# A hybrid attention layer: the output product moved to the end of the next tile, and the scale and shift of the input done token by token with a DMA transpose

## The chip, the cores and the metric

One NeuronCore of a Trainium2 chip runs the whole program. The metric is device microseconds of one execution. In the texts PE is TensorE (matrix products), DVE is VectorE, ACT is ScalarE, POOL is GpSimd, and SP is the engine whose queue issues the DMAs. A semaphore wait on an engine holds everything that stands behind it in that engine's program.

## What is computed

One layer over 4096 prompt tokens and 64 sample tokens, width 1024 (cut to what matters):

```python
shift, scale, gate = split(silu(c) @ w_ada + b_ada)
h = rmsnorm(x, g_pre) * (1 + scale) + shift
gq, gk, gv, gg, ga, sq, sk, sv, sg = split(h @ w_in)
o_gla = rmsnorm(gla_recurrence(q, k, v, log_a, S0), g) * silu(gg)
o_swa = sink_attention(rope(q), rope(k), v, window) * silu(sg)
o = concat(o_gla, o_swa) @ w_out
y = x + gate * rmsnorm(o, g_post)
```

## The kernel before

The prompt is cut into 32 tiles of 128 tokens (t = 0 to 31); tile 32 is the sample and step 33 only finishes it. Each engine has a `program(c)` that is run for each tile; tiles 0, 1 and 30 to 33 are written out, the rest is a loop over pairs of tiles (lines 251 to 259). All order is set by hand, by the order of instructions in each program and by semaphores.

Every large product is made of f16 halves: an operand is split into a high half (rounded to f16) and a low half (the rest), and `split_product` (line 425) adds high x high, high x low and low x high for each of the 8 chunks of the inner dimension: 24 matmuls at line 429. hT holds the two halves of h with channels on the partitions, for two tiles in turn. The products by h of a tile are qk (four blocks of 128), the 272-wide k/v/low-rank product into bank5, the SWA query product into bank7 and the GLA value product into bank6 (512 wide each), the GLA gate product gg into bank7 and the SWA gate product sg into bank6. The output product takes the mix of the previous tile and wo_hi, wo_lo: 48 matmuls into pairP.

PE's order in tile t (lines 492 to 646): qk of t; the GLA output and the state product of t-1 (lines 529 to 540); the 272-wide product; the product of probabilities and values of t-1 (PV, line 555); the query product; a small transpose of the low-rank part; the value product; z (line 578); the output product of t-1 (line 597); the scores (line 615); gg; eight transposes of the normalised x of tile t+1 into pairP (line 631); the transposes of k and the GLA block matrix A (lines 636 to 642); sg. So step t does the first half of tile t and the second half of tile t-1.

How h of tile t+1 comes about: ACT squares x and makes 1/rms (`x_stats`, line 667); POOL multiplies x by it into xs (`norm_x`, line 1131); PE transposes xs; DVE scales and shifts each of the eight channel blocks by columns of mod (`h_f32`, line 873), which also frees pairP; ACT writes the high half into hT (`h_hi`, line 700) and DVE the low half (`h_lo`, line 881).

The gates: ACT writes exp of the product into etmp, DVE adds 1, takes the reciprocal and multiplies by the product (lines 1091 to 1096 for gg, 1099 to 1111 for sg, both through the one buffer etmp). The softmax: DVE takes maxima of the scores (lines 1056 and 1057) and three small steps, ACT takes exponentials into late (line 811) and writes their high half into pair_tok (line 818), DVE the low half (line 1082). aT is lines 1076 to 1080. In line 1018 DVE copies a small column, in line 1060 it copies keys.

POOL (lines 1140 to 1199): copies of values, the rotary terms, `norm_x`, three GLA scalings, the residual add to y (line 1188), and a multiply of each gate half (lines 1193 and 1198).

SP's queue in order (lines 369 to 414): three DMA transposes of the mix from pair_tok into late (`turn_mix`), three of query and key halves (`turn_heads`), the store of y, a copy of x into x_res, the load of x for tile t+2, two transposes of the probabilities' halves (`turn_probs`). pair_tok carries first the mix, then the probabilities; the second half of late takes their transposes.

At the start, w_ada and w_in come in units through staging places, and ACT (`split_hi`) and DVE (`split_lo`) split each. The eight units of w_out pass through three places of stage (lines 53 and 112): units 0 to 2 are loaded in tile 0, units 3 to 5 behind tile 0's probabilities, 6 and 7 behind the mix of tile 1.

Of the kernel before, what the change touches and what calls it, by code (L numbers as in the profile page):

```python
# [12 lines left out]
P = 128  # L13
D = 1024
# [38 lines left out]
UNITS += [("out", i, 17 + i % 3) for i in range(OUT_UNITS)]  # L53
SLOTS = 20
SAME_PLACE = {17: (0, 17), 18: (1, 18), 19: (1, 19)}
# [16 lines left out]
class Tile:  # L72


    def __init__(self, t, half, par):
        peeled = isinstance(t, int)
        self.t, self.half, self.par = t, half, par
        self.prev = not (peeled and t == 0)
        self.cur = not (peeled and t == NT + 1)
        self.next = not (peeled and t >= NT)  # L80
        self.first = peeled and t == 0
        self.second = peeled and t == 1
        self.last = peeled and t == NT - 1
        self.sample = peeled and t == NT
        self.after = peeled and t == NT + 1


def hybrid_layer(nc, x_prompt, x_sample, c_prompt, c_sample, state_gla, cache_k, cache_v, w_ada, b_ada, g_pre,
# [3 lines left out]
    with ctx:  # L92
# [22 lines left out]
        gate_diag = y_buf[0].rearrange("p (c k) -> p c k", c=KC)  # L115
        first_diag = late[:, 0:D].rearrange("p (c k) -> p c k", c=KC)
        probs = late[:, 0:D].rearrange("p (g k) -> p g k", g=GROUPS)
        pair_tok = sb("pair_tok", [P, 2, D], F16)
        pair_ch = late[:, D:2 * D].bitcast(F16).rearrange("p (s c k) -> p s c k", s=2, c=KC)
# [7 lines left out]
        h_ch = xs[:, :].rearrange("p (c k) -> p c k", c=KC)  # L127
        hT = sb("hT", [P, 2, 2, KC, P], F16)
# [90 lines left out]
        u_ps = pairQ[:, 640:896].rearrange("p (b k) -> p b k", b=2)  # L219
# [14 lines left out]
        for name in ("c_load bg_load const_load c_t bg_t bg_ev rows_ev rows_t c_exp c_one c_rec c_silu eps_set "  # L234
                     "ident_z ident mask_z causal scan_z scan_m state_in gaT_one ga_lo w_al_hi w_al_lo mod_mm "
                     "mod_sum mod_out zeroed kcache_t cache_kA gdiag_d gate_bc gate_row x_sq x_lnd x_rs xs h_f32 "
# [29 lines left out]
        def _(sp):  # L266
# [58 lines left out]
            for n, (kind, i, slot) in enumerate(UNITS[:unit_number("out", 3)]):  # L325
# [43 lines left out]
            def program(c):  # L369
                if c.prev:  # L370
                    turn_mix(c)
                if c.second:
                    load_out((6, 7))
                if c.cur:
                    turn_heads(c)
                if c.last or c.sample:
# [7 lines left out]
                if c.prev:  # L384
                    sp.wait_ge(sem["y_final"], c.t)
                    src = y_buf[1 - c.par]
                    if c.after:
                        sp.dma_start(y_sample[0], src[0:DEC_SEQ, :]).then_inc(y_stored[1 - c.par], 16)
                    else:
                        sp.dma_start(y_prompt[0, bass.ds((c.t - 1) * P, P), :], src).then_inc(y_stored[1 - c.par], 16)  # L390
                if c.cur:
                    sp.wait_ge(x_loaded[c.par], 32 * (c.half + 1))
                    sp.dma_start(x_res[:, :], x_in[:, c.par, :]).then_inc(sem["res_copied"], 16)
                if not isinstance(c.t, int) or c.t + 2 <= NT:
                    sp.wait_ge(sem["res_copied"], 16 * (c.t + 1))
                    sp.wait_ge(sem["xs"], c.t + 1)
                    sp.wait_ge(sem["rope"], c.t + 1)
                    load_x(c.t + 2, c.par)
                if c.sample or c.after:
# [5 lines left out]
                if c.sample:  # L405
                    sp.wait_ge(sem["out_stored"], 16 * 4)
                    for q in range(2):
                        sp.dma_start(S[DK * q:DK * q + DK, :, q, :],
                                     state_gla[0, 0].rearrange("(b q) k v -> q k b v", q=2)[q])\
                          .then_inc(sem["state_in"], 16)  # L410
                if c.cur:
                    turn_probs(c)
                if c.first:
                    load_out((3, 4, 5))
# [9 lines left out]
        def _(pe):  # L424
# [58 lines left out]
            def gate_to_rows(count):  # L483

                pe.wait_ge(sem["gdiag_d"], count)
                diagonal = (first_diag, gate_diag)[count - 1]
# [3 lines left out]
                last.then_inc(sem["gate_bc"], 1)  # L490

            def program(c):
# [12 lines left out]
                if c.cur:  # L505
                    pe.wait_ge(sem["h_lo"], t + 1)
                    if c.first:
                        pe.wait_ge(sem["cache_kA"], 1)
                    else:
                        pe.wait_ge(sem["at_d"], t)  # L510
                    if c.first:
                        pe.wait_ge(w_split, in_units_before[W_QK])
# [6 lines left out]
                if c.prev:  # L519

                    pe.wait_ge(sem["at_d"], t)
                    pe.wait_ge(sem["gg_x"], t)
                    pe.wait_ge(sem["v_ev"], t)
                    if not c.second:
# [3 lines left out]
                    for b in range(2):  # L528
                        pe.matmul(bank7[:, 2 * b * DV:2 * (b + 1) * DV], q_int[:, b, :], S[:, b, :, :],
                                  start=True, stop=False)  # L530
                        for q in range(2):
                            o = slice((2 * b + q) * DV, (2 * b + q + 1) * DV)
                            last = pe.matmul(bank7[:, o], aT[:, b, q, :], v_tok[:, o], start=False, stop=(q == 1))
                    last.then_inc(sem["o_mm"], 1)

                    n = DEC_SEQ if c.after else P
                    pe.wait_ge(sem["p_exp"], t)
                    for hd in range(GH):
                        b, q = hd // 2, hd % 2
                        last = pe.matmul(u_ps[DK * q:DK * (q + 1), b, :], k_tok[0:n, b, DK * q:DK * (q + 1)],  # L540
                                         v_tok[0:n, hd * DV:(hd + 1) * DV], start=True, stop=True)
                    last.then_inc(sem["u_mm"], 1)
                if c.cur:
                    project(bank5, KSG, W_KSG, sem["ksg_mm"])
                if c.prev:
                    pe.wait_ge(sem["probs_dma"], 32 * t)
                    pe.wait_ge(sem["sg_x"], t)
                    pe.wait_ge(sem["v_keys"], t)
                    for g in range(KVH):
                        for ch in range(2):  # L550
                            v = vB[:, 1 - par, :, :] if ch else (vA_s if c.after else vA[:, 1 - par, :, :])
                            for pp in range(2):
                                k = 4 * g + 2 * ch + pp
                                for n, (i, j) in enumerate(((0, 0), (0, 1), (1, 0))):
                                    last = pe.matmul(bank6[:, k * HD:(k + 1) * HD], pair_ch[:, i, k, :],
                                                     v[:, j, HD * g:HD * (g + 1)], start=(n == 0), stop=(n == 2))
                    last.then_inc(sem["pv_mm"], 1)
                if c.cur:
                    if c.prev:
                        pe.wait_ge(sem["mix_gla"], t)  # L560
                    project(bank7, 512, W_SQ, sem["sq_mm"])
                    pe.wait_ge(sem["ksg_ev"], t + 1)
                    pe.wait_ge(sem["ga_lo"], t + 1)
                    pe.wait_ge(sem["vb_lo"], t + 1)
                    pe.transpose(gaT_ps, ga_pair[:, :], ident16[:, :]).then_inc(sem["gat_mm"], 1)
                if c.cur:
                    if c.first:
                        pe.wait_ge(sem["mod_sum"], 2)
                    if c.prev:
                        pe.wait_ge(sem["mix_swa"], t)  # L570
                    project(bank6, 512, W_V, sem["v_mm"])
# [8 lines left out]
                    last.then_inc(sem["z_mm"], 1)  # L580
                if c.prev:
                    pe.wait_ge(sem["mix_dma"], 48 * t)
                    if c.after:
                        pe.wait_ge(sem["gate_row"], 2)
                    else:
                        pe.wait_ge(sem["h_f32"], t + 1)
                    if c.second:
                        pe.wait_ge(w_split, len(IN_UNITS) + OUT_UNITS)

# [10 lines left out]
                if not c.cur:  # L600
                    return
                if c.first:
                    pe.wait_ge(sem["h_f32"], 1)
                    gate_to_rows(1)
                pe.wait_ge(sem["pair_dma"], 48 * (t + 1))
                pe.wait_ge(sem["k_ev"], t + 1)
                if c.prev:
                    pe.wait_ge(sem["s_upd"], t)
                for ch in range(2):
                    for pp in range(2):  # L610
                        for g in range(KVH):
                            kk = kB if ch else kA
                            head = 4 * g + 2 * pp
                            for part in range(2):
                                last = pe.matmul(scores[:, 4 * g + 2 * ch + pp, :],  # L615
                                                 qT[:, ch, head:head + 2, :], kk[:, g, part, :],
                                                 start=(part == 0), stop=(part == 1))
                last.then_inc(sem["sc_mm"], 1)
                pe.wait_ge(sem["sq_ev"], t + 1)
                project(bank7, 512, W_GG, sem["gg_mm"])  # L620
                if c.sample:
                    pe.wait_ge(sem["y_mul"], t)
                    gate_to_rows(2)
                if c.next:
                    pe.wait_ge(sem["xs"], t + 2)
                    if c.prev:
                        pe.wait_ge(sem["y_mul"], t)
                    else:
                        pe.wait_ge(sem["gate_row"], 1)
                    for cc in range(KC):  # L630
                        last = pe.transpose(pairP_c[:, cc, :], xs[:, cc * P:(cc + 1) * P], ident[:, :])  # L631
                    last.then_inc(sem["xt_mm"], 1)

                pe.wait_ge(sem["gla_sc"], t + 1)
                for b in range(2):
                    pe.transpose(kt_ps[:, b, :], k_out[:, b, :], ident[:, :])
# [600 lines left out]
```

## Time and profile before

| | us |
|---|---|
| three runs | 1714.31, 1716.46, 1716.52 (median 1716.46) |
| the profiled execution, its own time | 1715.52 |
| its span, first to last instruction | 1713.8 |
| PE busy | 1591.8 (93%) |
| DVE, ACT, POOL busy | 1079.0, 593.1, 365.1 |
| mean granted clock of PE | 0.983 |

Busy times are sums over an engine's instructions. A start in the timeline is when an instruction begins on its engine; matmuls overlap, so the next one begins before the last has ended, and the distance from start to start is what a stream of them costs. In brackets stands how long the engine was idle before an instruction, and what it waited for.

### The profile page before, as it was taken

How to read it: one execution, taken by the hardware profiler on the slowest of the kernel's cores; microseconds unless marked ns; L12 is line 12 of the kernel's file. 1: busy time of each engine (PE TensorE's matmuls, PEld its weight loads, DVE VectorE, ACT ScalarE, POOL GpSimd, SP SyncE). 2: the span in 40 equal slices, each digit the busy share in tenths (PEclk: the TensorE clock that was granted, in tenths of full speed). 3: DMA queues.
4: the chain of work that ended last, by engine and by line, in shares of the span. 5: the costliest groups of instructions: out<-in, count | busy, mean ns of one | idle time of the engine just before them, and what ended most of it. 6: DMA issues, size and time to landing. Idle time of an engine off the chain costs nothing.

```text
span 1713.8 us, 31107 instructions
## 1 busy us (share of the span) xinstructions
PE 1591.8 (93%) x12209; PEld 922.4 (54%) x12209; DVE 1079.0 (63%) x1937; ACT 593.1 (35%) x1812; POOL 365.1 (21%) x505
## 2 busy tenths in 40 slices
PE   8875999999999999999999999999999999999994
PEld 3442555555555555555555555555555555555552
DVE  0684676766666676766666676766666676776653
ACT  0543333333332333333332333333332333333331
POOL 0022222222222122222222121222222121222220
PEclk9988999999999999999999999999999999999997
DMA  8933232222212222222212222222221222222221
GB/s 262 333 87 81 72 72 61 59 70 71 71 47 45 71 71 62 61 68 71 71 50 42 71 71 63 62 65 71 71 54 40 68 71 64 62 64 65 62 53 36
DMA packets 242392, 128.96 MB, mean 75 GB/s; under 512 B 203709, under 2 KB 228758, under 8 KB 242358
## 3 DMA queue, kind: packets, MB, share of 16 engines
q1 hardware_dynamic: 242358, 128.51, 29.3%
q8 instruction: 22, 0.36, 0.1%
q14 instruction: 12, 0.10, 0.0%
HBM read 46.08 MB, written 17.56 MB: 37 GB/s over the span
## 4 chain that ended last, share of the span: by engine, by line
PE 54%; DVE 36%; SPq 3%; issue 3%; DMA 2%; ACT 2%; POOL 0%; DVEq 0%; ACTq 0%; POOLq 0%
PE bank L429 29%; PE pairP L429 20%; DVE etmp L1102 6%; DVE etmp L1094 6%; DVE xs L877 4%; DVE pair_tok L1082 2%; DVE gates L1109 2%; DVE hT L883 2%; DVE gates L955 2%; DVE etmp L1100 2%; PE pairQ L615 2%; SPq L310 2%; PE pairP L631 2%; DMA wo_lo<-in_w_in 1%; DVE aT L1076 1%
## 5 line engine op out<-in xcount | busy, mean ns | idle before, releaser
L429 PE MATMUL bank<-w_hi,hT 128*128 128x512 f16 (+1 forms) x2640 | 749.3, 360 | 8.5 <-DVE gates L955 8.1
L429 PE MATMUL bank<-w_lo,hT 128*128 128x512 f16 (+1 forms) x1320 | 474.7, 360 | 0.0
L429 PEld LDWEIGHTS bank<-w_hi,hT 128*128 128x128 f16 x2640 | 258.0, 98 | 265.9 <-DVE gates L955 11.9
L429 PE MATMUL pairP<-wo_hi,late 128*128 128x512 f16 x1056 | 323.3, 383 | 26.4 <-DVE wo_lo L865 17.2
L429 PE MATMUL bank<-hT,w_hi 128*128 128x128 f16 x2112 | 182.2, 220 | 29.5 <-DVE hT L883 24.4
L429 PE MATMUL pairP<-wo_lo,late 128*128 128x512 f16 x528 | 202.3, 383 | 0.0
L429 PEld LDWEIGHTS bank<-w_lo,hT 128*128 128x128 f16 x1320 | 129.3, 98 | 113.7 <-issue 0.6
L1033 DVE SCALAR_TENSOR_TENSOR stage<-pairP,y_r,stage 128x1024 f32<-128x1024 f32 x33 | 42.4, 1284 | 231.4 <-ACT y_r L665 231.4
L429 PEld LDWEIGHTS pairP<-wo_hi,late 128*128 128x128 f16 x1056 | 104.0, 98 | 153.3 <-issue 21.7
L429 PEld LDWEIGHTS bank<-hT,w_hi 128*128 128x128 f16 x2112 | 161.7, 98 | 45.3 <-DVE hT L883 40.1
L429 PE MATMUL bank<-hT,w_lo 128*128 128x128 f16 x1056 | 179.9, 220 | 0.0
L811 ACT ACTIVATE late<-pairQ,m_neg 128x128 f32<-128x128 f32 (+1 forms) x264 | 92.4, 375 | 140.5 <-DVE m_neg L1066 140.5
L1193 POOL TENSOR_TENSOR gates<-gates,gnorm 128x512 f32<-128x512 f32 x33 | 42.0, 1272 | 428.8 <-DVE gates L1096 428.8
L1188 POOL TENSOR_TENSOR stage<-stage,x_res 128x1024 f32<-128x1024 f32 x32 | 75.9, 2372 | 208.6 <-DVE stage L1033 208.6
L990 DVE TENSOR_TENSOR etmp<-qk_tok,etmp 128x512 f16<-128x512 f32 x33 | 22.8, 692 | 153.2 <-ACT junk L761 153.2
L1094 DVE RECIPROCAL etmp<-etmp 128x512 f32<-128x512 f32 x33 | 110.6, 3353 | 1.1
L1102 DVE RECIPROCAL etmp<-etmp 128x512 f32<-128x512 f32 x33 | 110.6, 3353 | 1.1
L1135 POOL TENSOR_TENSOR xs<-x_in,x_r 128x1024 f32<-128x1024 f32 x33 | 64.2, 1945 | 214.7 <-ACT x_r L663 214.7
L877 DVE TENSOR_SCALAR xs<-pairP,mod 128x128 f32<-128x128 f32 x264 | 87.1, 401 | 27.5 <-PE pairP L631 27.5
L429 PEld LDWEIGHTS bank<-hT,w_lo 128*128 128x128 f16 x1056 | 103.7, 98 | 0.0
L797 ACT ACTIVATE stage<-pairP 128x1024 f32<-128x1024 f32 x33 | 33.8, 1023 | 190.9 <-PE pairP L429 190.9
L832 ACT ACTIVATE etmp<-bank 128x512 f32<-128x512 f32 x33 | 19.7, 597 | 226.3 <-DVE gates L1096 226.3
(197 smaller groups left out, 2191.1 us busy)
## 6 DMA issues: line engine op xcount, KB each, us to landing
x_res<-x_in SPq DMA_DIRECT2D x33, 512.0 KB, 3.5
x_in<-in_x_prompt SPq DMA_DIRECT2D x32, 512.0 KB, 3.5
out<-stage SPq DMA_DIRECT2D x32, 512.0 KB, 2.7
w_hi<-in_w_ada SPq DMA_DIRECT2D x5, 1024.0 KB, 9.4
w_lo<-in_w_ada SPq DMA_DIRECT2D x5, 1024.0 KB, 13.2
wo_lo<-in_w_in SPq DMA_DIRECT2D x5, 1024.0 KB, 11.9
wo_hi<-in_w_in SPq DMA_DIRECT2D x3, 1024.0 KB, 12.4
late<-pair_tok SPq DMA_TRANSPOSE x165, 3.1
```

Of the source, the lines that this page charges most:

```text
L310: sp.dma_start(dst, src.rearrange("(c p) n -> p c n", p=P)).then_inc(staged[slot], 16)
L429: last = pe.matmul(out, a(c, i), b(c, j), start=(c == 0 and n == 0), stop=(c == KC - 1 and n == 2))
L615: last = pe.matmul(scores[:, 4 * g + 2 * ch + pp, :], qT[:, ch, head:head + 2, :], kk[:, g, part, :], start=(part == 0), stop=(part == 1))
L631: last = pe.transpose(pairP_c[:, cc, :], xs[:, cc * P:(cc + 1) * P], ident[:, :])
L811: act.activation(probs[:, g, 0:w], scores[:, g, 0:w], ACT.Exp, bias=m_neg[:, g:g + 1], scale=HD ** -0.5, accum_out=row_sum[:, g:g + 1])
L877: last = dve.tensor_scalar(h_ch[:, cc, :], pairP_c[:, cc, :], mod[:, KC + cc, cond:cond + 1], mod[:, cc, cond:cond + 1], ALU.mult, ALU.add)
L1033: dve.scalar_tensor_tensor(y_buf[1 - par], pairP[:, :], y_r[:, :], gate_row, ALU.mult, ALU.mult)\
L1094: dve.reciprocal(etmp[:, :], etmp[:, :]).then_inc(sem["gg_r"], 1)
L1102: dve.reciprocal(etmp[:, :], etmp[:, :]).then_inc(sem["sg_r"], 1)
L1135: pool.tensor_tensor(xs[:, :], x_in[:, par, :], x_r[:, par:par + 1].to_broadcast([P, D]), ALU.mult)\
L1188: pool.tensor_tensor(y_buf[1 - par], y_buf[1 - par], x_res[:, :], ALU.add).then_inc(sem["y_final"], 1)
L1193: pool.tensor_tensor(gg, gg, gnorm[:, :].unsqueeze(1).to_broadcast([P, GH, DV]), ALU.mult)\
```

## The change

Four things change together.

First, the order of step t on PE: qk of t, GLA output of t-1 (now into pairQ), the 272-wide product, the query product (into bank6), the small transpose, PV of t-1 (into pairQ), the state product of t-1, the value product (into bank7), z, gg (bank6), sg (bank7), scores, the k transposes and A, and last the output product of t-1. DVE and ACT programs are reordered to match: gg's gate stands before the maxima, sg's gate after aT, the y of t-2 is scaled at the start of the step, and x_stats of t+1 comes first on ACT.

Second, h of tile t+1 is made with tokens on the partitions. Three rows (scale, shift, gate), broadcast over the partitions, are made at the start by the diagonal product that made the gate row before; scale lies in xs, shift in stage. POOL makes h in three operations in late, ACT and DVE write its halves into pair_tok, and two DMA transposes put them into hT. Tile 32's h is still made by PE's transposes, in step 31.

Third, POOL and SP: `make_h` stands first in POOL's step, then the residual add of y of t-2, then the rotary terms and the value copies. SP's order is: store of y of t-2, x_res loaded from the input in HBM, transposes of h, of heads, load of x for t+2, transposes of the mix, and transposes of the probabilities, which wait for the output product.

Fourth, w_out's units pass through two places of stage instead of three, as shift takes the third. Units 0 and 1 are loaded in tile 0, and three more pairs in tile 1.

```diff
-UNITS += [("out", i, 17 + i % 3) for i in range(OUT_UNITS)]
+UNITS += [("out", i, 18 + i % 2) for i in range(OUT_UNITS)]
...
+        shift_row = stage[:, D:2 * D]
+        h_tok = late[:, 0:D]
+        scale_row = xs[:, :]
+        o_ps = pairQ[:, 0:512]
+        pv_ps = pairQ[:, 512:1024]
...
             def turn_probs(c):
+                if c.prev:
+                    sp.wait_ge(sem["out_mm"], c.t)
...
+            def turn_h(c):
+                for part, done in enumerate(("h_hi", "h_lo")):
+                    sp.wait_ge(sem[done], c.t + 2)
+                    if c.prev and part == 0:
+                        sp.wait_ge(sem["sg_mm"], c.t)
+                    sp.sem_inc(sem["h_turn"], 1)
+                    sp.dma_start_transpose(hT[:, 1 - c.par, part, :, :], pair_tok[:, part, :]).then_inc(sem["h_dma"], 16)
...
             def program(c):
+                if c.prev2:
+                    sp.wait_ge(sem["y_final"], c.t - 1)
+                    sp.dma_start(y_prompt[0, bass.ds((c.t - 2) * P, P), :], y_buf[c.par]).then_inc(y_stored[c.par], 16)
                 if c.prev:
-                    turn_mix(c)
...
+                        sp.dma_start(x_res[:, :], x_prompt[0, bass.ds((c.t - 1) * P, P), :])\
+                          .then_inc(sem["res_copied"], 16)
                 if c.second:
-                    load_out((6, 7))
+                    load_out((2, 3))
+                if c.next and c.prev and not c.last:
+                    turn_h(c)
                 if c.cur:
                     turn_heads(c)
+                if c.second:
+                    load_out((4, 5))
...
+                if c.prev:
+                    turn_mix(c)
+                if c.second:
+                    load_out((6, 7))
...
PE
-                    pe.wait_ge(sem["h_lo"], t + 1)
+                    if c.first or c.sample:
+                        pe.wait_ge(sem["h_lo"], t + 1)
+                    else:
+                        pe.wait_ge(sem["h_dma"], 32 * t)
...
+                    pe.wait_ge(sem["sq_ev"], t + 1)
+                    project(bank6, 512, W_GG, sem["gg_mm"])
+                    pe.wait_ge(sem["v_ev"], t + 1)
+                    project(bank7, 512, W_SG, sem["sg_mm"])
...
                 if c.prev:
                     pe.wait_ge(sem["mix_dma"], 48 * t)
...
+                        pe.wait_ge(sem["y_mul"], t - 1)
...
ACT
+            def h_tok_hi(c):
+                act.wait_ge(sem["h_f32"], c.t + 2)
+                if c.prev:
+                    act.wait_ge(sem["probs_dma"], 32 * c.t)
+                act.activation(pair_tok[:, 0, :], h_tok, ACT.Copy).then_inc(sem["h_hi"], 1)
...
+                    if c.next and not c.last:
+                        act.wait_ge(sem["h_dma"], 32 * (t + 1))
                     act.activation(mix_tok[:, :, 0, :], gates[:, :].rearrange("p (f k) -> p f k", f=2), ACT.Copy)\
...
DVE
+            def h_tok_lo(c):
+                dve.wait_ge(sem["h_hi"], c.t + 2)
+                dve.tensor_tensor(pair_tok[:, 1, :], h_tok, pair_tok[:, 0, :], ALU.subtract).then_inc(sem["h_lo"], 1)
...
POOL
+            def make_h(c):
+                t, par = c.t + 1, 1 - c.par
+                pool.wait_ge(sem["x_rs"], t + 1)
...
+                    pool.wait_ge(sem["p_lo"], t - 1)
+                pool.tensor_tensor(h_tok, x_in[:, par, :], x_r[:, par:par + 1].to_broadcast([P, D]), ALU.mult)\
+                    .then_inc(sem["xs"], 1)
+                pool.wait_ge(sem["xs"], t + 1)
+                pool.tensor_tensor(h_tok, h_tok, scale_row, ALU.mult).then_inc(sem["h_a"], 1)
+                pool.wait_ge(sem["h_a"], t)
+                pool.tensor_tensor(h_tok, h_tok, shift_row, ALU.add).then_inc(sem["h_f32"], 1)
```

## Rows read from the trace of the kernel before

**Rows 1.** The page's head.

```profile
span 1713.8 us, 31107 instructions
```

**Rows 2.** Windows, one steady tile: stretch, length, busy of each engine, granted clock, DMA.

```profile
805.65:853.78 48.13, 46.39 (x363) 27.23 (x364) 31.41 (x58) 16.97 (x54) 10.88 (x15) 1.00 0.26 64
```

**Rows 3.** Timeline of PE in that tile: start, length, instruction, idle before.

```profile
816.19 0.28 PE L429 MATMUL bank<-w_hi,hT 128*128 128x272 f16 x1
817.20 0.34 PE L555 MATMUL bank<-vA,late 128*128 128x64 f16 x6 [0.73 <-issue]
...
818.31 0.39 PE L429 MATMUL bank<-w_hi,hT 128*128 128x512 f16 x1 [0.25 <-DVE gates L955]
...
829.37 0.39 PE L429 MATMUL pairP<-wo_hi,late 128*128 128x512 f16 x1
...
839.74 0.61 PE L615 MATMUL pairQ<-kA,qT 128*128 128x128 f16 x8
...
845.81 1.04 PE L631 MATMUL pairP<-ident,xs 128*128 128x128 f32 x8
846.68 0.38 PE L636 MATMUL bank<-ident,la 128*128 128x128 f32 x2
...
852.64 0.38 PE L429 MATMUL bank<-w_hi,hT 128*128 128x512 f16 x1
853.78 0.28 PE L429 MATMUL bank<-hT,w_hi 128*128 128x128 f16 x2 [0.76 <-DVE hT L883]
```

**Rows 4.** Timeline of DVE, the same tile and the seam behind it.

```profile
832.69 1.87 DVE L1018 COPY fac_in<-bsum 128x2 f32<-128x2 f32 x1
...
843.02 0.68 DVE L1056 TENSOR_REDUCE smax<-pairQ 128x4 f32<-128x512 f32 x1
...
846.01 0.17 DVE L1068 TENSOR_TENSOR sink_d<-sinks,m_neg 128x8 f32<-128x8 f32 x1
...
849.45 0.40 DVE L1076 TENSOR_TENSOR aT<-bank,causal 64x256 f32<-64x256 f32 x1
...
851.36 1.23 DVE L1082 TENSOR_TENSOR pair_tok<-late,pair_tok 128x1024 f16<-128x1024 f32 x1
...
859.16 0.91 DVE L1100 TENSOR_SCALAR etmp<-etmp 128x512 f32<-128x512 f32 x1 [0.72 <-ACT etmp L832]
...
865.26 1.13 DVE L955 SCALAR_TENSOR_TENSOR gates<-bank,o_r,gates 128x128 f32<-128x128 f32 x4
```

**Rows 5.** Timeline of POOL there.

```profile
832.59 1.94 POOL L1135 TENSOR_TENSOR xs<-x_in,x_r 128x1024 f32<-128x1024 f32 x1 [6.04 <-ACT x_r L663]
...
843.27 2.34 POOL L1188 TENSOR_TENSOR stage<-stage,x_res 128x1024 f32<-128x1024 f32 x1 [6.43 <-DVE stage L1033]
...
865.30 1.04 POOL L1198 TENSOR_TENSOR gates<-gates,rden 128x512 f32<-128x512 f32 x1 [5.52 <-DVE gates L1109]
```

**Rows 6.** SP's queue: two transposes, and the landing of those at line 355.

```profile
872.25 2.58 SPq L347 DMA_TRANSPOSE late<-pair_tok  x2
...
DMA to landing us min/median/max: 3.0/3.3/5.1
```

**Rows 7.** Timelines of start and end: PE, SP's queue and ACT.

```profile
143.77 2.40 SPq L317 DMA_DIRECT2D stage<-in_w_out  x4
...
150.74 1.06 ACT L689 ACTIVATE wo_hi<-stage 128x1024 f16<-128x1024 f32 x1 [1.15 <-DMA stage<-in_w_out]
...
153.19 0.59 PE L429 MATMUL pairP<-wo_hi,late 128*128 128x512 f16 x1 [17.16 <-DVE wo_lo L865]
...
179.92 0.28 PE L429 MATMUL bank<-hT,w_hi 128*128 128x128 f16 x2 [0.76 <-DVE hT L883]
...
1623.90 0.29 PE L429 MATMUL bank<-hT,w_hi 128*128 128x128 f16 x2 [0.76 <-DVE hT L883]
...
1664.06 1.88 PE L488 MATMUL pairP<-stage,causal 128*128 128x512 f32 x4
...
1692.53 0.61 PE L429 MATMUL pairP<-wo_hi,late 128*128 128x512 f16 x1 [9.27 <-DMA late<-pair_tok]
```

More of the change, by code:

```diff
@@ new lines, in program @@
+                    for ch in range(2):
+                        for pp in range(2):
+                            for g in range(KVH):
+                                kk = kB if ch else kA
+                                head = 4 * g + 2 * pp
+                                for part in range(2):
+                                    last = pe.matmul(scores[:, 4 * g + 2 * ch + pp, :],
+                                                     qT[:, ch, head:head + 2, :], kk[:, g, part, :],
+                                                     start=(part == 0), stop=(part == 1))
@@ L599, in program @@
                     last.then_inc(sem["out_mm"], 1)
[L600 to L632, printed above, removed]
@@ L800, in program @@
-                if not c.cur:
-                    return
-                if c.first:
-                    split_hi([("in", 11)])
-                act.wait_ge(sem["m_neg"], t + 1)
-                if c.prev:
-                    act.wait_ge(sem["p_lo"], t)
-                if c.first:
-                    act.wait_ge(sem["zeroed"], 1)
-                for g in range(GROUPS):
-                    w = CHUNK if c.first and g % 4 < 2 else P
-                    act.activation(probs[:, g, 0:w], scores[:, g, 0:w], ACT.Exp, bias=m_neg[:, g:g + 1],
-                                   scale=HD ** -0.5, accum_out=row_sum[:, g:g + 1])
@@ new lines, in program @@
+                    act.wait_ge(sem["m_neg"], t + 1)
+                    if c.last:
+                        act.wait_ge(sem["xt_mm"], 2)
+                    elif c.sample:
+                        act.wait_ge(sem["p_lo"], t)
+                    else:
+                        act.wait_ge(sem["h_lo"], t + 2)
+                    if c.first:
+                        act.wait_ge(sem["zeroed"], 1)
+                    for g in range(GROUPS):
+                        w = CHUNK if c.first and g % 4 < 2 else P
+                        act.activation(probs[:, g, 0:w], scores[:, g, 0:w], ACT.Exp, bias=m_neg[:, g:g + 1],
+                                       scale=HD ** -0.5, accum_out=row_sum[:, g:g + 1])
@@ new lines, in program @@
+                    act.wait_ge(sem["sink_d"], t + 1)
+                    act.activation(sink_e[:, :], sink_d[:, :], ACT.Exp).then_inc(sem["p_exp"], 1)
+                    act.wait_ge(sem["p_exp"], t + 1)
+                    if c.prev:
+                        act.wait_ge(sem["mix_dma"], 48 * t)
+                    else:
+                        act.wait_ge(sem["h_dma"], 32)
+                    act.activation(pair_tok[:, 0, :], late[:, 0:D], ACT.Copy).then_inc(sem["p_hi"], 1)
+                    if c.first:
+                        split_hi([("out", 0), ("out", 1)])
@@ L1111, in program @@
-                last.then_inc(sem["sg_x"], 1)
             all_tiles(dve, program, 2)
```

524 lines of the change are left out of this document (283 added, 241 removed).

## The prediction

> **What bounds the kernel now.** I read the profile's page first: a span of 1713.8 us [rows 1]. Its own time is 1715.52 us, so 1.7 lie around the span; it is 0.9 below the median of 1716.46, and I work against 1715.5. Then one steady tile by windows: 48.13 us, TensorE (PE) busy 46.39, VectorE (DVE) 31.41, ScalarE (ACT) 16.97, GpSimd (POOL) 10.88, granted clock 1.00 [rows 2]. PE is the bound; no other engine is near. Tile 2 begins at 179.92 and tile 32 at 1623.90 [rows 7]: 30 tiles of (1623.90 - 179.92) / 30 = 48.13. What a tile saves counts thirty times.
>
> Then PE's timeline of such a tile, to see what in 48.13 isn't products. It stands still three times: 0.73 before PV (L555), 0.25 before the SWA query product, 0.76 before the next tile's first product [rows 3], 1.74 in all. Each is more from start to start, as the pipe drains too. The 48 products of the output product start over 839.74 - 829.37 = 10.37 us, 0.216 each; the last gate product starts at 852.64 and could be followed at 852.86, but the next comes at 853.78: 0.92. The 272-wide product takes 0.115 apiece in proportion, so 816.30 to 817.20 is 0.90. Add 0.41 for the third (its 0.25 and a like drain). Sum 2.23. All three wait for DVE: at the tile's seam stands its gate chain, 6.10 long (859.16 to 865.26, [rows 4]) and there twice, which holds the banks and the gates.
>
> **The change, part by part.** *PE, removed.* Eight transposes of x, 846.68 - 845.81 = 0.87 a tile [rows 3]. Everything else is the same products in another order.
>
> *PE, the stalls.* T is the start of a tile's first product. Without stalls a tile is 48.13 - 2.23 - 0.87 = 45.03. The low end of the stalls by the tags alone, 1.74, gives 45.52. I take 45.05, as the drain is lost only when PE really waits. Is the new order free of waits? It ends with the output product, 10.37 long, so that starts at T+34.7. Ahead of it lie kt and A (first gate product 852.64 - 23 x 0.216 = 847.67, less 846.68: 0.99) and the scores (845.81 - 24 x 0.216 = 840.63, less 839.74: 0.89). So the last gate product ends at T+32.8 and the scores at T+33.7: 11.3 us of products cover what used to be the seam.
>
> *DVE behind that.* From T+33.7: maxima and their small successors 846.18 - 843.02 = 3.16 (with the waiting copy in it), aT 1.91 (849.45 to 851.36), the gate chain 6.10, then the probabilities' low half 1.23 [rows 4]. Finished at T+44.8 (gates) and T+46.1, which is 1.0 into the next tile. The next tile first needs those gates for its value product at T+16.7 and the transposed low half for PV at T+15.4. The h halves and aT are needed at T and T+5.4 of the next tile and are there many microseconds before. So the three stalls go, and I find none in their place on this side. h as eight DVE operations per tile goes too; it costs nothing in either kernel, as DVE has 16 us to spare a tile.
>
> *The new chain.* h of tile t+1 is now POOL, ACT, DVE, two DMA transposes; pair_tok holds it, then the mix, then the probabilities. POOL's gate multiply (1.04) ends at T+2.4; then x times 1/rms (1.95) and two products with a full second operand (2.35 each by the residual add, [rows 5]): T+9.1. The y add follows, T+11.4; before, it stood after the GLA scaling. ACT takes the high half after the k/v evictions: PE's 272-wide product ends at T+10.1 (816.30 - 805.65 less 0.6 for the state product moved behind PV), so T+10.7 to 11.8 with 1.06, as L689, of the same shape, takes [rows 7]. DVE's low half, 1.2, is done at T+13.0. SP is queued behind POOL's y add: y store and x_res load are issued at T+11.5 to 12.3, then two transposes at 1.29 each [rows 6]. The second goes out at T+13.6 and lands 3.3 later, T+16.9 (worst seen 5.1: T+18.7). ACT's mix high half waits for that, and the head split behind it on ACT, and the value eviction behind that; the value product ends only at T+22.0. PE does the query product (5.2), the small transpose and PV (0.7) after T+10.1, so PV ends at T+16.1 and its DVE multiply at T+16.8: the mix would not be there earlier anyway. Mix high half T+18.0, low half T+19.2, head low halves T+20.3. SP: three head transposes until T+24.2, the x load 0.8, three mix transposes, the last issued at T+27.6 and landing at T+30.9. The output product wants it at T+34.7: 3.8 to spare. With both landings at their worst (1.8 more each) 0.2 is left. I take no cost; ends are 0 and, if landings are all at the worst and 1 us more is lost in the queue, 0.8 a tile. The GLA scaling (qk_d at T+27) and the scores' heads (T+26) have 5 and more.
>
> *DMA.* Two more transposes a tile, 10 instead of 8, and x_res comes from HBM, no more than it took before; SP issues for some 15 of 45 us. Hidden.
>
> *The port.* DVE's copy L1018 is 1.87 long under POOL's x multiply (832.59 to 834.53), while four gate multiplies from PSUM run at their usual 1.13 beside POOL's 1.04 [rows 4, 5]. So some DVE operations wait for a POOL one to end and some don't. The Trainium skill, SBUF - State Buffer, section "SBUF: two separate sides", says that the port pair is locked for a whole instruction, and that a DVE operation with two SBUF inputs loses it to GpSimd as well. The trace agrees for L1018; the rule speaks against the change, which gives POOL 4.7 us more a tile. In the times above, POOL's block T+2.4 to 11.4 meets only DVE work that reads PSUM, and L1018 and the k copy fall free of POOL. If the block slips onto h's or the mix's low half, 2.35 a time is lost in the chain with 3.8 to spare.
>
> *Tile 31* keeps its PE transposes: 0.9 back.
>
> *The start.* Weights bound it. Before, the output product of tile 1 waited 17.16 for wo_lo [rows 7]. Now that product stands later in its tile, but w_out passes through two staging places instead of three, and the loads stand behind h and head transposes on SP. Tile 1 starts at about 112 as before. By the same durations (estimates, each step from the one before): tile 0's last gate multiply on POOL 123.9, h on POOL 130.7, h halves 133, splits of units 0 and 1 135.5, loads 2 and 3 with h's transposes 142, splits 146.4, head transposes 151.3, loads 4 and 5 (7.0 from first issue to both landed, 143.77 to 150.74, [rows 7]) 158, splits 160, loads 6 and 7 167, last split 169.6, output product 180. ACT blocks on the staged units, so the value eviction and the last gate product wait there too. Tile 2 at 180 against 179.92: 0, with ends of -10 (half of the stall saved) and +10 (one more round of 7 and a slow clock).
>
> *The tail.* From 1623.90 to the end 89.9. Now: the tile without stalls 45.05, probability transposes 4.7, PV and multiply 1.4, mix halves 3.4, three mix transposes 5.3, shift of the gate row (1.88, [rows 7], and a copy of 1) 3: output product at 62.9; after it 1713.8 - 1692.53 = 21.3 as before: 84.2. Saves 5.7.
>
> **Sum.** 30 x (48.13 - 45.05) = 92.4, less 0.9, plus 5.7, start 0: 97. 1715.5 - 97 = 1618.5; I say **1619**. The stalls at the tags' size alone: 30 x 0.47 = 14 more, 1633.
>
> **Rivals.** *A, no waits left on PE* (above): 1605 to 1640. For it: every wait in the new order has microseconds of cover. Against it: the chain through five units is longer than any now. Chance 0.68.
>
> *B, the h and mix chain is late by a little:* the output product stands 1 to 2 us in each tile, 1619 + 30 to 60 = 1649 to 1679. For: SP's fixed order puts h behind the y add. Against: 3.8 spare. 0.12.
>
> *C, POOL and DVE block each other:* by the rows' mechanism POOL's 9 us block slides under the low halves and each lengthens the other; two such waits of 2.35 are 4.7, less 3.8 spare is 0.9 a tile: 1646. The Trainium skill (SBUF - State Buffer, the same section) would have it so wherever these operations meet. 0.08.
>
> *D, slower:* the two added transposes, behind 1 MB of store and load, land late in every tile. The price is what exceeds 3.8; it outweighs the gain of 3.1 only from 6.9 us on. At 9 a tile costs 5.2 - 3.1 = 2.1 more than before: 1715 + 63 = 1778. Against: the probability transposes go out right behind an x load and land in 3.3, 5.1 at most [rows 6]. 0.07.
>
> *E, the change doesn't do what it says:* the seam's waits come back elsewhere at the same size (DVE's gate chain before the value product, say), and only the transposes are saved: 30 x 0.87 = 26, 1689; with the start at +10 and a chain 0.5 late, no change. 0.05, of which 0.02 ends within 0.2%.
>
> **How the numbers follow.** A measurement can tell some 0.2% (3.4 us) from no change. Faster: A, B, C and most of E, 0.91; same 0.02; slower 0.07. The range takes A with both bounds of start and stalls, C and the near half of B: 1604 (start -10, tail 5 better) to 1662. Outside lie the rest of B, D and E, under 0.2.
>
> **What would show it.** Right: PE's tile at 45.0 to 45.5, no idle before PV and the query product, output product following kt and A at once, DVE's L1018 far below its 1.87, PE transposes of x in the loop gone but for tile 31's eight, tile 32 some 92 us earlier. B: PE's wait before the output product, named as the DMA into late. C: POOL's three h operations or DVE's low halves above their 2.35 and 1.2. D: transposes landing after 10 us. The forecast is wrong if PE's tile is over 46.5.

## The result and the profile after

The changed kernel takes 1623.76 us, median of four runs (1623.61 to 1624.17); the kernel before, on the same chip, 1716.18 (1714.31 to 1716.52). The ratio is 0.9464, 95% interval 0.9448 to 0.9480: 92 us less. The forecast was 1619 within 1604 to 1662.

The page of the changed kernel, where its span and chain stand:

```profile
span 1621.9 us, 30679 instructions
...
PE 1555.8 (96%) x11969; PEld 901.3 (56%) x11969; DVE 934.3 (58%) x1691; ACT 593.9 (37%) x1814; POOL 543.5 (34%) x567
...
PE 85%; DVE 2%; SPq 2%; DMA 1%; issue 1%; ACT 0%; POOL 0%; POOLq 0%; ACTq 0%
```

The last line gives the shares of the chain that ends last. In the kernel before it read:

```profile
PE 54%; DVE 36%; SPq 3%; issue 3%; DMA 2%; ACT 2%; POOL 0%; DVEq 0%; ACTq 0%; POOLq 0%
```

So PE went from 54% of the chain to 85%, and DVE from 36% to 2%. What the chain still holds of other engines should lie where PE waits. These are the waits of PE that recurred in the kernel before, as line, releaser, total, times and longest:

```profile
PE bank L555 <- issue: 27.5, 33, 4.2
PE bank L429 <- DVE hT L883: 24.4, 32, 0.8
...
PE bank L429 <- DVE gates L955: 8.1, 32, 0.3
```

And these are the three longest waits of the changed kernel:

```profile
PE bank L457 <- ACT v_tok L832: 17.5, 1, 17.5
PE bank L457 <- DVE w_lo L927: 11.0, 2, 7.2
PE pairP L516 <- DMA late<-pair_tok: 8.0, 1, 8.0
```

None of its waits occurs more than twice: apart from 1.65 in tile 2 they lie in the start and the tail. A steady tile by windows (span; busy of PE, PEld, DVE, ACT, POOL; clock; DMA share; GB/s), to be set beside [rows 2]:

```profile
726.00:771.07 45.07, 45.07 (x358) 26.54 (x357) 26.55 (x49) 16.97 (x54) 16.73 (x18) 1.00 0.33 79
```

PE is busy in all of it. DVE fell by 4.9 us, POOL rose by 5.9. The timeline gives the rest (other rows left out): the first products of tiles 1, 2, 14, 15 and 32 on PE, the output product of step 2, and, within the steady tile 14, rows of each unit of the new chain:

```profile
119.24 0.27 PE L457 MATMUL bank<-hT,w_hi 128*128 128x128 f16 x2 [3.34 <-DVE k_tok L1154]
184.10 0.27 PE L457 MATMUL bank<-hT,w_hi 128*128 128x128 f16 x2
220.45 0.39 PE L457 MATMUL pairP<-wo_hi,late 128*128 128x512 f16 x1 [1.65 <-DMA late<-pair_tok]
...
725.97 0.28 PE L457 MATMUL bank<-hT,w_hi 128*128 128x128 f16 x2
731.27 2.35 POOL L1226 TENSOR_TENSOR late<-late,stage 128x1024 f32<-128x1024 f32 x1
736.51 1.07 ACT L758 ACTIVATE pair_tok<-late 128x1024 f16<-128x1024 f32 x1
737.61 1.23 DVE L956 TENSOR_TENSOR pair_tok<-late,pair_tok 128x1024 f16<-128x1024 f32 x1 [0.57 <-ACT pair_tok L758]
737.69 3.07 SPq L372 DMA_TRANSPOSE hT<-pair_tok  x2
743.07 1.06 ACT L815 ACTIVATE pair_tok<-gates 128x1024 f16<-128x1024 f32 x1 [1.03 <-DVE gates L1051]
749.36 1.26 SPq L383 DMA_TRANSPOSE kB<-junk  x1
753.17 2.59 SPq L354 DMA_TRANSPOSE late<-pair_tok  x2
760.61 0.39 PE L457 MATMUL pairP<-wo_hi,late 128*128 128x512 f16 x1
...
770.98 0.28 PE L457 MATMUL bank<-hT,w_hi 128*128 128x128 f16 x2
...
1537.08 0.28 PE L457 MATMUL bank<-hT,w_hi 128*128 128x128 f16 x2
```

Tile 2 to tile 32 takes 1537.08 - 184.10 = 1352.98 where it was 1443.98 [rows 7]: 91.0 less. The start is 184.10 - 179.92 = 4.2 longer. The tail is 1621.9 - 1537.08 = 84.8, where it was 89.9: 5.1 less. 91.0 - 4.2 + 5.1 = 91.9, the difference of the two spans. From tile to tile it is 45.01; the 30 hold two exceptions, tile 2 (46.7, with its one wait of 1.65) and tile 31 (45.9, with its eight transposes).

The two rows to read together are L815 and L372. The mix's high half (L815) waited for DVE's gates, done at 742.96, and not for the two h transposes issued from 737.69 on. Their landing, in the same tile:

```profile
DMA to landing us min/median/max: 3.6/3.8/4.1
```

The second was issued at 739.05 and landed 3.6 later, at 742.66, so only 0.3 ahead of the gates. In tiles 4 to 29 it lands at T+16.5 to T+17.2 (T is the start of the tile's first product), and the mix's high half starts at T+17.1 to T+17.2 in all of them: the two paths are even. The room lies behind them. The mix transposes land at T+31.3 to T+31.6, 3.0 to 3.4 before the output product at T+34.6. So h passes through five units in the shadow of other work, as the sum needed.

### The profile page after: what moved, and what is told of

The parts are those of the page before. It is cut to its first block, busy times and chain, and to the rows that moved or that the text cites. A ratio compares the mean times of both kernels' runs of the same rounds, so it can differ in the third digit from the quotient of the medians.

```text
span 1621.9 us, 30679 instructions
## 1 busy us (share of the span) xinstructions
PE 1555.8 (96%) x11969; PEld 901.3 (56%) x11969; DVE 934.3 (58%) x1691; ACT 593.9 (37%) x1814; POOL 543.5 (34%) x567
## 4 chain that ended last, share of the span: by engine, by line
PE 85%; DVE 2%; SPq 2%; DMA 1%; issue 1%; ACT 0%; POOL 0%; POOLq 0%; ACTq 0%
PE bank L457 54%; PE pairP L457 21%; PE pairQ L562 2%; PE pairQ L638 2%; PE pairQ L566 2%; PE pairQ L599 2%; PE pairQ L607 1%; PE bank L620 1%; DMA hT<-pair_tok 1%; DMA late<-pair_tok 1%; PE bank L648 1%; PE bank L644 0%; PE bank L649 0%; DVE wo_lo L923 0%; SPq L354 0%
## 5 line engine op out<-in xcount | busy, mean ns | idle before, releaser
L457 PE MATMUL bank<-w_hi,hT 128*128 128x512 f16 (+1 forms) x2640 | 741.7, 361 | 28.5 <-ACT v_tok L832 17.5
L1288 POOL TENSOR_TENSOR gates<-gates,rden 128x512 f32<-128x512 f32 x33 | 35.2, 1067 | 336.6 <-DVE rden L1175 336.6
L1027 DVE SCALAR_TENSOR_TENSOR gates<-pairQ,o_r,gates 128x128 f32<-128x128 f32 x132 | 37.2, 344 | 179.2 <-ACT o_r L693 179.2
L1246 POOL TENSOR_TENSOR rope_cos<-qk_tok,trig_in 128x80 f32<-128x80 f32 x33 | 12.1, 368 | 265.7 <-issue 184.2
L1274 POOL TENSOR_TENSOR k_off<-k_d,fac 128x128 f32<-128x128 f32 x33 | 13.2, 401 | 252.6 <-DVE k_d L1102 252.6
L779 ACT ACTIVATE junk<-pairQ 128x128 f16<-128x128 f32 x132 | 34.6, 277 | 167.6 <-PE pairQ L566 167.6
L457 PEld LDWEIGHTS pairP<-wo_lo,late 128*128 128x128 f16 x528 | 51.9, 98 | 58.8 <-issue 0.8
```

Source lines behind the costliest of these rows:

```text
L457: last = pe.matmul(out, a(c, i), b(c, j), start=(c == 0 and n == 0), stop=(c == KC - 1 and n == 2))
L779: last = act.activation(junk[:, hd * DV:(hd + 1) * DV], o_ps[:, hd * DV:(hd + 1) * DV], ACT.Square, accum_out=o_ss[:, hd:hd + 1])
L1027: last = dve.scalar_tensor_tensor(gates[:, o], o_ps[:, o], o_r[:, hd:hd + 1], gates[:, o], ALU.mult, ALU.mult)
L1288: pool.tensor_tensor(sg, sg, rden[:, :].unsqueeze(2).to_broadcast([P, GROUPS, HD]), ALU.mult)\
```

## The experiments

In each, the kernel before ran on the same chip. Seven kernels were run.

**The order alone.** The new order stays; h goes the old way.

```
 PE, after the 272-wide product, tiles 1 to 31 (was: tile 31 only)
-                    if c.last:
+                    if c.next and c.prev:
                         pe.wait_ge(sem["xs"], t + 2)
...
                         for cc in range(KC):
                             last = pe.transpose(pairP_c[:, cc, :], h_tok[:, cc * P:(cc + 1) * P], ident[:, :])
 DVE
-                    h_f32(2, 1)
+                    h_f32(t + 1, 1 if c.last else 0)
 SP
-                if c.next and c.prev and not c.last:
-                    turn_h(c)
```

> The changed kernel with its new tile order kept, but scale and shift of tile t+1 made the old way in all tiles after the first: eight TensorE transposes, VectorE's scale and shift behind them, ScalarE's and VectorE's halves straight into hT, no transposes by DMA. Theory (the order takes the seam waits away; the DMA transposes only take eight transposes off TensorE): 30 tiles grow by the 0.9 us that tile 31 of the changed kernel pays for them, so 1624 + 27 = 1651 us, 1645 to 1657, with no TensorE wait of note in a steady tile. Rival (the token-major h chain took the waits away, and the order alone leaves them): up to the 48.1 us tile of the kernel before, 1690 to 1716 us.

Measured 1642.68 us (1641.16 to 1643.86), ratio 0.9572 [0.9556, 0.9588]. A steady tile of it by windows:

```profile
731.20:777.09 45.89, 45.89 (x365) 27.38 (x364) 29.18 (x57) 17.09 (x54) 11.97 (x16) 1.00 0.27 66
```

PE is busy throughout here too, with the long h chain on DVE (29.18). So the order takes the waits away: 48.13 - 45.89 = 2.24 a tile. Making h token-major and turning it by DMA then takes off another 45.89 - 45.01 = 0.88. That is the theory, and per tile it is exact; the total missed its lower bound of 1645, because the expectation carried the tile's term and forgot the start. Tile 2 begins at 180.56 here and at 184.10 in the changed kernel, and tile 2's wait of 1.65 is absent. The token-major h of tiles 2 to 31 (that of tile 1 is token-major in both) therefore costs 3.5 us at the start and 1.65 in tile 2, which 29 tiles of 0.88 have to pay for: 25.5 - 5.2 = 20.3, against 1642.0 - 1621.9 = 20.1 between the two profiles.

**The gate chain of the kernel before, shortened.**

```
-                dve.reciprocal(etmp[:, :], etmp[:, :]).then_inc(sem["gg_r"], 1)
+                dve.reciprocal(etmp[:, 0:8], etmp[:, 0:8]).then_inc(sem["gg_r"], 1)
...
-                dve.reciprocal(etmp[:, :], etmp[:, :]).then_inc(sem["sg_r"], 1)
+                dve.reciprocal(etmp[:, 0:8], etmp[:, 0:8]).then_inc(sem["sg_r"], 1)
```

> The kernel before with both gate reciprocals of VectorE cut from 512 to 8 columns; this leaves out the gates' reciprocals, and nothing else is moved. Theory (the seam waits of the kernel before are VectorE's gate chain, two reciprocals of 3.35 us in it): the waits at the values' product and at the first product go, the tile falls from 48.13 us to between 45.9 and 46.4, so 1716 - 30 x 1.7 to 2.2 = 1650 to 1665 us. Rival (the waits come from somewhere else, a transfer or TensorE's own order): 1710 to 1716 us.

Measured 1665.75 us (1664.09 to 1666.16), ratio 0.9711 [0.9694, 0.9727]. Its steady tile by windows, and its longest entry among PE's waits:

```profile
737.81:784.63 46.82, 46.05 (x363) 27.25 (x364) 25.13 (x58) 16.98 (x54) 10.87 (x15) 1.00 0.26 65
```

```profile
PE bank L429 <- DVE hT L883: 24.5, 32, 0.8
```

Half right. The waits before PV and before the query product are gone, 48.13 - 46.82 = 1.31 a tile, 39 us in 30. But the tile is slower than the 45.9 to 46.4 expected, and the total comes to within 1 us of its range only because the start and the tail gave 4.0 and 8.1, which the expectation did not count. The 0.77 before the first product stands in all 32 tiles still: DVE is late there too, with h's low half (L883), which stands ahead of the gate chain in DVE's order. So of the 2.23 that the prediction read off [rows 3], 1.31 belong to the gates and 0.92 to h. The prediction put them all down to the gate chain; the change takes both away, so the sum did not notice.

**The reciprocals of the changed kernel, shortened.** The same two lines.

> The changed kernel with both gate reciprocals of VectorE cut from 512 to 8 columns; this leaves out the gates' reciprocals. Theory (in the steady tiles VectorE's gate chain lies wholly beside the output product now, so TensorE alone bounds them): steady tile 45.0 us as before the cut, the time 1615 to 1624 us, the difference at the start alone. Rival (VectorE still bounds part of the tile): 1 us a tile or more, 1594 us or less.

Measured 1620.14 us (1615.99 to 1620.38), ratio 0.9435 [0.9421, 0.9449]. Two tile starts:

```profile
724.37 0.28 PE L457 MATMUL bank<-hT,w_hi 128*128 128x128 f16 x2
769.39 0.28 PE L457 MATMUL bank<-hT,w_hi 128*128 128x128 f16 x2
```

45.02 a tile with 6 us less on DVE. The same cut that gave the kernel before 50 us gives this one 3.6, none of it in a steady tile: between the two profiles it is 1.7 in tile 2, whose wait is gone, and 1.7 in the tail, and not at the start, where the expectation put it. In the steady tiles DVE is off the path.

**The output product put back ahead of the scores.**

```
-                    (scores, kt and A)
                 if c.prev:
                     pe.wait_ge(sem["mix_dma"], 48 * t)
...
                     last.then_inc(sem["out_mm"], 1)
+                if c.cur:
+                    (scores, kt and A)
```

> The changed kernel with the output product put back ahead of the scores and the two small products behind them, all else as it is. Theory (the 10.4 us of the output product behind the scores are what covers VectorE's and ScalarE's work at the seam): the first product of a tile waits at least the 3.3 us for k_tok that tile 1 of the changed kernel shows, and the probabilities and with them h come 5 us later, so 3.3 to 5.5 us a tile, 1624 + 100 to 165 = 1724 to 1789 us. Rival (the position of the output product is worth nothing, the shorter h chain is): 1619 to 1630 us.

Measured 1931.85 us (1927.54 to 1939.20), ratio 1.1251 [1.1234, 1.1268]: 308 us more than the changed kernel, nearly twice the theory's upper bound of 165. Three windows of a tile (the whole tile; its first product up to the output product's wait; the output product), and the two waits:

```profile
851.69:906.67 54.98, 48.55 (x355) 28.47 (x356) 26.82 (x50) 16.82 (x56) 15.86 (x17) 0.94 0.28 65
851.69:886.24 34.55, 34.55 (x265) 21.65 (x265) 20.06 (x37) 14.10 (x42) 14.59 (x16) 0.95 0.36 89
...
889.66:902.00 12.34, 12.34 (x54) 5.43 (x55) 0.00 (x0) 0.36 (x1) 1.02 (x1) 0.86 0.00 0
```

```profile
889.66 0.39 PE L457 MATMUL pairP<-wo_hi,late 128*128 128x512 f16 x1 [3.42 <-DMA late<-pair_tok]
...
906.67 0.27 PE L457 MATMUL bank<-hT,w_hi 128*128 128x128 f16 x2 [3.01 <-DVE k_tok L1155]
```

And from the chain of h in the same tile:

```profile
867.82 2.19 DVE L957 TENSOR_TENSOR pair_tok<-late,pair_tok 128x1024 f16<-128x1024 f32 x1 [3.43 <-ACT pair_tok L759]
870.21 3.67 SPq L372 DMA_TRANSPOSE hT<-pair_tok  x2
```

Both expected waits are there: 3.0 at the seam, and 3.4 for the mix, since POOL's h waits for the probabilities' low half, which now come after the seam. They make 6.4. The other 3.5 of 54.98 - 45.01 are clock: the first stretch takes 34.55 where the same products take 32.76 in the changed kernel, at a granted clock of 0.95, and the output product 12.05 (its first product at 889.66, the scores at 901.71) where it takes 10.37, at 0.86, so part of each ran at 1.2 instead of 2.4 GHz, each right behind one of the waits. The theory named both waits, took the second 1 us too short and left the clock out. SP's order has a part in the second, the reason that the prediction gave for rival B: the first h transpose is issued 2.4 after the high half is written (at 867.79), behind the store of y, which waits for POOL's add of y; in the changed kernel it is issued 0.1 after. Beside that add (866.57 to 868.93) DVE's low half of h takes 2.19 instead of 1.23, which is rival C's case; it is done before the queue is free for it. With the rest of the new order, the position of the output product is worth 10 us a tile, far more than the 2.2 that the old order lost; why the old order lost so little without it was not tried.

**How much the chain has to spare.** Each h transpose of tiles 4 to 29 is issued once or twice more, ahead of the real one.

```
 SP, turn_h
+                    if not isinstance(c.t, int):
+                        extra(c, part)
                     sp.dma_start_transpose(hT[:, 1 - c.par, part, :, :], pair_tok[:, part, :]).then_inc(sem["h_dma"], 16)
 extra: the same transpose into x_in's dead half, in the second kernel also into the dead y buffer
```

> The changed kernel with each of the two h transposes of tiles 4 to 29 issued a second time, into a buffer that is dead then, ahead of the real one: 2.5 us more on the SP queue between h and mix in 26 tiles. Theory (the chain h, mix, mix transposes has 3.4 us to spare before the output product): no change, 1622 to 1628 us; the mix halves come about 2 us later and the mix transposes land about 1.4 us before the output product. Rival (the chain is late already, or blocks another queue): 2.5 us a tile, 1624 + 65 = 1689 us.

> The same with each h transpose of tiles 4 to 29 issued twice more: 5 us more on the SP queue. Theory (3.4 us to spare): 1.1 to 1.7 us a tile are now missing, 1624 + 29 to 44 = 1653 to 1668 us, with TensorE waiting ahead of the output product for the mix transposes' landing. Rival (no spare): 5 us a tile, 1754 us. Rival (the queue's order hides it, or there is far more to spare): 1624 us.

Once more: 1622.51 us (1621.16 to 1623.79), ratio 0.9457 [0.9441, 0.9472], no change. The mix's high half of one tile (first product at 725.64) is now released by the h transposes, at T+19.3 instead of T+17.1:

```profile
744.90 1.06 ACT L826 ACTIVATE pair_tok<-gates 128x1024 f16<-128x1024 f32 x1 [3.19 <-DMA hT<-pair_tok]
```

Twice more: 1684.53 us (1681.18 to 1693.34), ratio 0.9832 [0.9799, 0.9866], 61 us more than the changed kernel. The 29 to 44 expected were too few. PE's waits, windows of two tiles and of the output product of the second, and the rows of the first:

```profile
PE pairP L470 <- DMA late<-pair_tok: 45.9, 27, 2.6
```

```profile
700.48:747.10 46.62, 45.08 (x356) 26.49 (x355) 25.91 (x50) 16.74 (x54) 15.48 (x17) 1.00 0.44 99
747.10:795.80 48.70, 46.76 (x356) 26.86 (x355) 25.99 (x50) 16.74 (x54) 16.89 (x19) 0.96 0.43 94
...
783.75:795.80 12.05, 12.05 (x48) 5.11 (x49) 10.15 (x20) 5.86 (x23) 2.35 (x3) 0.86 0.00 0
```

```profile
722.72 1.06 ACT L828 ACTIVATE pair_tok<-gates 128x1024 f16<-128x1024 f32 x1 [6.17 <-DMA hT<-pair_tok]
736.73 0.39 PE L470 MATMUL pairP<-wo_hi,late 128*128 128x512 f16 x1 [1.54 <-DMA late<-pair_tok]
```

The mechanism is as told: the only wait that comes in tile after tile is the mix transposes' landing. The mix came 22.24 after the tile's start instead of 17.10, 5.14 later, and PE waited 1.54: 3.6 to spare, where the prediction had 3.8. The waits sum to 45.9, a little above the expected range. Another 14.6 are in PE's busy time (1570.4 on its page against 1555.8), which the expectation left out. The second tile shows how: its wait was 1.94, and the output product behind it took 12.05 at a granted clock of 0.86, while behind the 1.54 it took the usual 10.37. Eight of the 26 output products were so slowed, by 13.2 together.

**The ends reordered.** From the waits of PE: what is left lies at the start and in the tail. The idea is that the order of the queues makes it.

```
 PE, tail
+                    if c.after:
+                        pe.wait_ge(sem["y_mul"], t - 1)
+                        gate_to_rows(4)
                     pe.wait_ge(sem["mix_dma"], 48 * t)
 tile 0: POOL make_h ahead of rope; ACT x_stats(1) behind gate_to_stage(2);
         splits of in 8, 9 ahead of the head halves, of 10, 11 ahead of h's halves
 tile 1: SP    load_out((4, 5)) ahead of turn_heads, load_out((6, 7)) ahead of turn_mix
         ACT   split_hi of 2, 3 ahead of the mix, of 4, 5 behind z's Ln, of 6, 7 behind the gate's Exp
         DVE   split_lo of 0, 1 first in the tile, 2, 3 behind h's low half, 4, 5 and 6, 7 as ACT's
```

> The changed kernel with its start and its end reordered, its 30 steady tiles untouched. Tile 0: statistics and h of tile 1 made ahead of GpSimd's rope, the input weights' units 8 to 11 split ahead of the attention heads and of h's halves. Tile 1: w_out's units 0 to 7 loaded and split each one step earlier in SP's, ScalarE's and VectorE's order, behind the v copy instead of ahead of it. End: the sample's gate row product ahead of the wait for the mix transposes. Theory (the three waits at the ends hang on queue order alone): tile 1 starts 5 to 9 us earlier than at 119.2 us, tile 1 takes 8 to 12 us less than 64.9, the tail falls by 4.9 us; 1624 - 18 to 26 = 1598 to 1606 us. Rival (the transfers themselves bound the start): only the tail's 4.9 us, 1619 us.

Measured 1603.14 us (1603.07 to 1603.57), ratio 0.9344 [0.9332, 0.9357]: 20.6 us under the changed kernel, the fastest of all. Its PE rows at both ends:

```profile
114.95 0.37 PE L457 MATMUL bank<-hT,w_hi 128*128 128x128 f16 x2 [3.33 <-DVE k_tok L1150]
157.07 0.59 PE L457 MATMUL pairP<-wo_hi,late 128*128 128x512 f16 x1 [4.59 <-DVE wo_lo L921]
169.79 0.28 PE L457 MATMUL bank<-hT,w_hi 128*128 128x128 f16 x2
...
1572.74 3.78 PE L516 MATMUL pairP<-stage,causal 128*128 128x512 f32 x4
1580.82 0.61 PE L457 MATMUL pairP<-wo_hi,late 128*128 128x512 f16 x1 [4.30 <-DMA late<-pair_tok]
```

Tile 1 starts 4.3 us earlier (5 to 9 expected, a miss: POOL's rope, now behind h, kept ACT waiting 5.0, and two of its six operations took 2.40 instead of 0.35 beside DVE's splits of weights). Tile 1 takes 169.79 - 114.95 = 54.8 instead of 64.9, and the 17.5 us wait is gone. The gate row product runs while the mix transposes are under way, and the tail, 1601.4 less tile 32's start at 1521.06, is 80.3 instead of 84.8. Tile 2's 1.65 went as well. 14.3 + 1.7 + 4.5 = 20.5. So much of what was left hung on queue order; what each of the moves gave was not tried.

## Why the prediction was right

**PE's stalls.** Predicted: 2.23 of waits and drain gone, tile 45.05 (45.52 by the tags alone). Measured 45.01 from start to start, and the order alone 2.24. Counting from start to start rather than by the tags was right, and worth 14 us of the forecast. Which work they waited for was only partly right: 1.31 was the gate chain and 0.92 the low half of h. That the sum came out all the same is in this part luck, as the change took both away.

**PE's transposes.** 0.87 predicted, 0.88 measured with the order held fixed; tile 31 keeps its own, as said.

**DVE behind the scores.** Gates at T+44.8 and the low half at T+46.1 predicted; the gate rows end 43.2 and the low half 44.4 after the tile's start. L1018's stalled copy (1.87 in [rows 4]) is now 0.16, out of POOL's way, as foretold.

**The new chain.** Predicted and measured, from T: h on POOL 9.1 and 7.7; high half 11.8 and 11.6; low half 13.0 and 12.9; mix high half 18.0 and 18.2; heads issued till 24.2 and 24.6; output product 34.7 and 34.6. The step that decided was "3.8 to spare" at no cost. It is 3.0 to 3.4 by the landings and 3.6 by the two extra transposes, and 2.5 us more in the queue cost nothing. So rival B, which needed the chain 1 to 2 late, and D, whose transposes had to come 6.9 late, fall. So does E: no wait of a steady tile came back elsewhere.

**The port, rival C.** Its sign did not show in the steady tile: POOL's h operations take 2.36 and DVE's low halves of h and the mix 1.23 at most. A smaller case of it happened and cost nothing. POOL's value copy (0.39 when free) and DVE's low halves of the mix and the heads meet. The heads' two, 0.69 and 0.42 when free, become 0.88 and 0.61, and POOL's copy 1.21:

```profile
744.16 1.23 DVE L1061 TENSOR_TENSOR pair_tok<-gates,pair_tok 128x1024 f16<-128x1024 f32 x1
744.42 1.21 POOL L1260 COPY vA<-vB 64x256 f16<-64x256 f16 x1 [0.28 <-POOL qk_tok L1252]
745.30 0.88 DVE L1067 TENSOR_TENSOR etmp<-qk_tok,etmp 128x512 f16<-128x512 f32 x1
746.11 0.61 DVE L1068 TENSOR_TENSOR junk<-qk_tok,junk 128x256 f16<-128x256 f32 x1
```

0.4 us in a chain with 3.6 to spare. The rule of the Trainium skill that the prediction weighed (SBUF - State Buffer, "SBUF: two separate sides") agrees.

**The start, mis-sized.** "Tile 1 starts at about 112 as before" failed: it starts at 119.24. The prediction moved h of tile 1 onto POOL and pair_tok at the start but priced only tile 1's weight loads. Two things were left out. Tile 0 has no output product that could cover its seam, so the first product of tile 1 waits 3.34 for k_tok, where in the kernel before it waited 0.76 for h. And in tile 0, DVE's split of the last input weights, for which PE waits 7.2, stands behind h's halves, and DVE's work before it was held up by POOL's h (last section). How the 7.5 divide was not measured; with the ends reordered, which changes only the second, tile 1 starts 4.3 earlier and still waits 3.33. From there the estimated round of loads and splits was 3 us too long (64.9 for tile 1 where 68 was worked out), so tile 2 came at 184.1 against 180. The bounds of 10 either way held both.

**The tail.** 84.2 predicted, 84.8 measured. The shift of the gate row behind the mix was seen and priced at 3; the trace has 4.9 from 1596.33 to 1601.22, as its product is 3.78 long, at a granted clock of 0.50, the lower of the two levels (1.2 GHz).

In all, 97 saved was forecast and 92 came: start -4.2 instead of 0, tile 2 -1.65, tail 0.6 short, against 30 tiles that came out 0.04 better each.

## What to carry to other kernels

Where PE is near its bound and waits at a seam for another engine, look for a long product that does not depend on the seam, and put it there: 10.4 us of output product covered what cost 6.4 us of waits and 3.5 of clock when it stood elsewhere. Count a stall from start to start, not by its tag. And when the steady part is done, read the waits that occur once: here 20 us lay in the order of loads, splits and one product at the ends, and reordering them was worth a fifth of the change itself.

## What was not expected of the hardware

A short wait can cost its length twice. In the kernel that issues each h transpose twice more, PE waited ahead of the output product in each of the 26 tiles. In eight of them, behind waits of 1.92 to 2.57, the product took 11.8 to 12.1, with a granted clock of 0.86 in the one shown: up to 1.7 more. In the other 18 it took 10.37. Fifteen of those waits were of 1.21 to 1.81, but three were of 2.02, 2.33 and 2.52, so the length of the wait alone does not decide. What else does was not tried.

POOL's wide operations can hold DVE's small ones for their own length. In tile 0 of the changed kernel three DVE operations run beside POOL's h:

```profile
92.90 1.93 DVE L1081 TENSOR_TENSOR_SCAN bsum<-scan_mask,la 128x256 f32<-128x256 f16 x1
94.36 2.61 POOL L1224 TENSOR_TENSOR late<-late,xs 128x1024 f32<-128x1024 f32 x1
94.86 2.39 DVE L1086 TENSOR_TENSOR q_d<-bsum 128x256 f32<-128x256 f32 x1
97.05 2.42 POOL L1226 TENSOR_TENSOR late<-late,stage 128x1024 f32<-128x1024 f32 x1
97.17 2.31 DVE L1091 COPY fac_in<-bsum 128x4 f32<-128x4 f32 x1
```

In a steady tile the same three lines take 0.69, 0.42 and 0.16; here 6.6 us for 1.3, with even a copy of four columns nearly as long as POOL's 128x1024. The Trainium skill (SBUF - State Buffer, "SBUF: two separate sides") says that where an operation of each contends for the port pair that they share, the later one is blocked until the first has ended. These rows agree. This time it lies in the work that leads to the weight split for which PE waits 7.2. In the kernel with its ends reordered, POOL's h stands elsewhere, and they take 0.69, 0.42 and 0.16 again.
